# Three norms of a decoder trunk: the last tile's squares are added on VectorE and summed by one product, a step later

## The chip, the cores and the metric

The kernel runs on one core of one Trainium2 chip. The metric is the device time of one execution in microseconds (us), as the median of several runs. A profiled execution of the same kernel gives the trace: for every instruction its engine, its line in the kernel, its start and its length.

Engines are named as in the trace: PE is TensorE's matmuls and PEld its weight loads, DVE is VectorE, ACT is ScalarE, POOL is GpSimd, SP is SyncE.

## What is computed

A trunk of two decoder layers over 512 tokens of width 1024: a gated short convolution, a squared-ReLU MLP, then an attention layer that reads a shared key/value cache, and a second MLP. Each part starts with an RMS norm over the 1024 channels. Three of these norms matter here: the one before the first MLP (norm 1), the one before the shared keys and values (norm 2) and the one before the second MLP (norm 3).

```python
def rms_norm(x, g):
    xf = x.astype(jnp.float32)
    y = xf * lax.rsqrt(jnp.mean(xf * xf, axis=-1, keepdims=True) + EPS)
    return y.astype(x.dtype) * g
...
        x = x + g_m[:, None, :] * y
        h = modulate(rms_norm(x, norm_mlp_g[l]), sh_f, sc_f)
        x = x + g_f[:, None, :] * squared_relu_mlp(h, mlp_w1[l], mlp_w2[l])
        if l == N_A - 1:
            k, v, F = shared_kv(x, kv_norm_g, w_kv, k_norm_g, w_f, b_f)
```

## The kernel before

**Layout.** Channels lie on the 128 partitions, so `x` is eight tiles of 128 channels by 512 tokens, and a sum over channels is a sum over the eight tiles and over the partitions. Every dense product is made in three matmuls of rounded parts (`products`, lines 734 to 736): high weights by high activations, high by low, low by high. Each weight block therefore needs a high part (ScalarE, line 1299) and a low part (VectorE, line 1828), and so does each tile of `h` (`h_hi` from ScalarE, `h_lo` from VectorE).

**A norm in two token halves.** To keep TensorE at work across a norm, the last three blocks (`SPLIT = 3`) of the dense stage ahead of it are computed for tokens 0 to 255 first, then for tokens 256 to 511, and so is the norm. For each half ScalarE squares a tile into `tb` and VectorE adds it to `ssum` (`half_add`, line 1921). The last tile's squares are not added: `norm_sum` multiplies `ssum` by a matrix of ones (line 773) and then `tb`, which holds the last squares, by the same ones (line 775), both unrounded float32 into one bank. This gives every partition the sum over all channels. ScalarE then makes the root by a logarithm and an exponential (`norm_root`, line 1331 and the two after it), VectorE refines it (`norm_end`, lines 1857, 1860 and 1861), scales the tiles (line 1873, in norm 2 line 1886), ScalarE writes the high part and VectorE the low part (line 1882, in norm 2 line 1891).

**The order on TensorE.** `first_blocks` takes the stage behind the norm. For the first half it runs k from 0 to 10: at k it gives block 0 its tile k (`step(0, half, k)`, three matmuls of 128x256) and block 1 its tile k-3. Each step waits until that tile's low part is there (`h_ok`). At k = 5, ahead of the step, stands `norm_sum(n, 1)`, the sum of the second half. Then comes a third block over the first half (24 matmuls), and only then the steps of the second half, which need the second root. In norm 2 block 0 is the forget gate's (`wf_hi`, `wf_lo`).

**The order on VectorE.** `norm_in_halves` runs, for each half, low part m, then the scaling of tile m+2. In the first half it puts in the updates of `x` for the second half (line 1912, after m = 0, 2, 4) and the additions of squares (line 1921, after m = 2 and 4). After m = 7 it waits for the second root. In norm 1 and 2 the low part of the third or the next weight block (line 1828) stands behind the first two scalings of the second half; norm 2 has another one ahead of `norm_end`.

**The order on ScalarE.** `norm_in_halves` there runs the high parts of the 16 half tiles, with the squares of the second half ahead of m = 2, 4 and 6, and the second root ahead of m = 8.

All queues run in program order; semaphores join them.

Of the kernel before, what the change touches and what calls it, by code (L numbers as in the profile page):

```python
# [23 lines left out]
ALU = mybir.AluOpType  # L24
# [6 lines left out]
KT = D // P  # L31
# [77 lines left out]
def yoco_trunk(nc, x_in, c_in, ada_w, ada_b, norm_mix_g, norm_mlp_g, sc_w_in, sc_conv, sc_w_out,  # L109
# [13 lines left out]
    def new(name, shape, dt):  # L123
        offset = top[0]
        top[0] += size(shape, dt)
        return at(name, shape, dt, offset)
# [6 lines left out]
    def stacked(offset, specs):  # L133
        made = []
        for name, shape, dt in specs:
            made.append(at(name, shape, dt, offset))
            offset += size(shape, dt)
        return made
# [46 lines left out]
    ssum = new("ssum", [P, T], F32)  # L185
# [4 lines left out]
    tb, = stacked(region_tb, [("tb", [P, 2, T], F32)])  # L190
# [15 lines left out]
    ones = new("ones", [P, P], F32)  # L206
# [9 lines left out]
    cols = new("cols", [P, ROWS], F32)  # L216
# [58 lines left out]
    with ExitStack() as ctx:  # L275
# [3 lines left out]
        def sem(name):  # L279
            return ctx.enter_context(nc.semaphore(name))  # L280
# [39 lines left out]
        half_done = sem("half_done")  # L320
        half_ok = sem("half_ok")
        sq_half = sem("sq_half")
        ss_ok = sem("ss_ok")
        norm_pe = sem("norm_pe")
        norm_y = sem("norm_y")
# [75 lines left out]
        HALF = [slice(0, T // 2), slice(T // 2, T)]  # L401
        HALF_OUT = [slice(0, T), slice(T, 2 * T)]
        ALL = slice(0, T)
        SPLIT = 3
        SQ = [None] + [n * (KT - 1 + SPLIT - 1) for n in range(3)]

        def norm_no(n, half):

            return 2 * n - 1 + half if n else 0
# [320 lines left out]
        def _(pe):  # L730
            mm, turn = nc.tensor.matmul, nc.tensor.transpose

            def products(out, weights_hi, weights_lo, hi, lo, k, cols=ALL):
                mm(out[:, cols], weights_hi, hi[:, k, cols], start=(k == 0), stop=False)  # L734
                mm(out[:, cols], weights_hi, lo[:, k, cols], start=False, stop=False)  # L735
                return mm(out[:, cols], weights_lo, hi[:, k, cols], start=False, stop=(k == KT - 1))  # L736

            def part_of(b, s, out, hi, lo, tiles, ready=None, cols=ALL, weights=(w_hi, w_lo)):

                pe.wait_ge(lo_ok, b + 1)  # L740
                for k in tiles:
                    if ready:
                        ready(k)
                    last = products(out, weights[0][:, s, k, :], weights[1][:, s, k, :], hi, lo, k, cols)
                return last
# [21 lines left out]
            def norm_sum(n, half):  # L767

                out, cols = bank[4][:, 0:T // 2], HALF[half]
                pe.wait_ge(ss_ok, SQ[n] + KT - 1 + half * (SPLIT - 1))  # L770
                if half:
                    pe.wait_ge(norm_v, norm_no(n, 0) + 1)
                mm(out, ones[:], ssum[:, cols], start=True, stop=False)
                pe.wait_ge(sq_half, norm_no(n, half))
                mm(out, ones[:], tb[:, 1 - half, cols], start=False, stop=True).then_inc(norm_pe, 1)
# [22 lines left out]
            def first_blocks(base, targets, n, third):  # L798


                def step(which, half, k):
                    out, weights_hi, weights_lo, done, split_at = targets[which]
                    pe.wait_ge(h_ok, base + half * KT + k + 1)
                    if k == 0 and half == 0:
                        pe.wait_ge(*split_at)
                        if which:
                            pe.wait_ge(half_ok, SPLIT * (n - 1) + 1)
                    last = products(out, weights_hi(k), weights_lo(k), h_hi, h_lo, k, HALF[half])
                    if half and k == KT - 1:
                        last.then_inc(done, 1)  # L810

                for half, lag in ((0, 3), (1, 3)):
                    for k in range(KT + lag):
                        if half == 0 and k == 5:
                            norm_sum(n, 1)
                        if k < KT:
                            step(0, half, k)
                        if k >= lag:
                            step(1, half, k - lag)
                    if half == 0:  # L820
                        b, out = third
                        pe.wait_ge(half_ok, SPLIT * (n - 1) + 2)
                        part_of(b, b % GROUP, out, h_hi, h_lo, range(KT), cols=HALF[0])
# [991 lines left out]
        def _(dve):  # L1815
            steps = [0]
            tt, stt, ts = nc.vector.tensor_tensor, nc.vector.scalar_tensor_tensor, nc.vector.tensor_scalar
# [97 lines left out]
            def half_add(n, half, i):  # L1915

                m = SQ[n] + KT - SPLIT + i + half * (SPLIT - 1)
                dve.wait_ge(sq_ok, m + 1)
                dve.wait_ge(ss_ok, m)
                cols = HALF[half]  # L1920
                tt(ssum[:, cols], ssum[:, cols], tb[:, (i + 1 + half) % 2, cols], ALU.add).then_inc(ss_ok, 1)

            def norm_in_halves(n, b, layer, part, scale, low):

                half_tile(n, 0, SPLIT - 1, b, layer, part)
                half_add(n, 0, SPLIT - 2)
                if n == 1:
                    ada_step(b // GROUP, b % GROUP, KT - 1, 5)
                    split((b + 2) // GROUP, (b + 2) % GROUP)
                if n == 3:  # L1930
                    split((b + 3) // GROUP, (b + 3) % GROUP)
                norm_end(n, 0, HALF[0])
                for half in range(2):
                    first = half * KT
                    for m in range(first, first + 2):
                        scale(m, m % KT, HALF[half])
                    if half and n != 3:
                        split((b + 3) // GROUP, (b + 3) % GROUP)
                    for m in range(first, first + KT):
                        low(m, m % KT, HALF[half])  # L1940
                        if m in (0, 2, 4):
                            half_tile(n, 1, m // 2, b, layer, part)
                        if m in (2, 4):
                            half_add(n, 1, m // 2 - 1)
                        if m + 2 < first + KT:
                            scale(m + 2, (m + 2) % KT, HALF[half])
                    if half == 0:
                        if n == 2:
                            split((b + 2) // GROUP, (b + 2) % GROUP)
                        norm_end(n, 1, HALF[1])  # L1950
# [257 lines left out]
            def mlp(layer, first, g_base):  # L2208
# [39 lines left out]
                with dve.Fori(1, CH - 1) as c:  # L2248
# [9 lines left out]

            mlp(0, MLP0, G_MLP0)
            norm_in_halves(2, KVQ - 1, 0, 5, lambda m, j, part: times_rms(H_KV + m, j, part),  # L2260
                           lambda m, j, part: kv_low(H_KV + m, j, part))

# [306 lines left out]
            for c in range(LAST):  # L2569
                n, nxt, last = GROUP * (c + 1), c + 1, c == LAST - 1  # L2570
# [80 lines left out]
```

## Time and profile before

| | us |
|---|---|
| median of 3 runs | 1168.93 |
| lowest and highest | 1168.38, 1169.27 |
| profiled execution, device time | 1169.95 |
| its span in the trace | 1168.2 |
| PE busy | 1150.4 |
| DVE busy | 872.1 |
| ACT busy | 547.1 |

The profiled execution took 1.02 us more than the median, and 1.75 us of it lie outside the span. A row of the trace below has the start in us from the start of the span, the length, the engine, the line, the operation and its output and inputs. Matmuls overlap: the length of one includes filling and emptying the array, so the pace is read from one start to the next. The same holds on VectorE and ScalarE, where the next operation often starts a little before the end of the one ahead.

### The profile page before, as it was taken

Reading aid. Unit: us, or ns where it says so; the run is one execution under the profiler, and the core shown is the slowest. Engines: PE = TensorE matmul, PEld = TensorE weight load, DVE = VectorE, ACT = ScalarE, POOL = GpSimd, SP = SyncE. Lnnn points to the kernel's source line nnn. Section 1 sums busy time; section 2 is a strip of 40 time slices with the busy share of each in tenths; the row PEclk is TensorE's granted clock in tenths of the full one; section 3 lists DMA queues with packets and bytes.
Section 4 is the critical chain, followed back from the end, with each engine's and each line's share of the span. In section 5 each row is a group of like instructions: output and inputs, shape, how many; then the busy total and the mean of one; then the engine's idle time right before and its main releaser. Section 6 shows DMA issues by size and latency. Waiting matters only on the chain.

```text
span 1168.2 us, 16194 instructions
## 1 busy us (share of the span) xinstructions
PE 1150.4 (98%) x5751; PEld 965.3 (83%) x5751; DVE 872.1 (75%) x1188; ACT 547.1 (47%) x874; POOL 25.2 (2%) x37
## 2 busy tenths in 40 slices
PE   6999999999999999999999999999999999999998
PEld 4788888988888888888978888888988888888887
DVE  5656888886675675545889888897887777769694
ACT  5422333642232241233678778774675344545521
POOL 2000000000000000200020000000000000000000
PEclk9999999999999999999999999999999999999999
DMA  9767566376666656333255455464033323332311
GB/s 327 249 184 251 172 206 199 109 216 197 189 189 197 198 179 198 109 91 90 64 136 132 123 131 139 111 163 142 24 106 124 95 88 109 108 113 86 109 55 72
DMA packets 200987, 168.87 MB, mean 145 GB/s; under 512 B 5620, under 2 KB 173724, under 8 KB 200924
## 3 DMA queue, kind: packets, MB, share of 16 engines
q1 hardware_dynamic: 200732, 167.92, 48.1%
q8 instruction: 38, 0.62, 0.2%
q14 instruction: 25, 0.20, 0.1%
q10 hardware_dynamic: 160, 0.06, 0.0%
q0 software_dynamic: 32, 0.07, 0.0%
HBM read 153.24 MB, written 2.10 MB: 133 GB/s over the span
## 4 chain that ended last, share of the span: by engine, by line
PE 91%; DVE 5%; ACT 2%; issue 1%; DMA 1%; SPq 0%; DVEq 0%; ACTq 0%
PE bank L734 23%; PE bank L736 23%; PE bank L735 23%; PE bank L991 4%; PE bank L989 4%; PE bank L990 4%; PE bank L1141 1%; PE bank L1159 1%; PE bank L1131 1%; PE bank L1132 1%; DMA x_rows<-in_x 1%; PE bank L866 1%; DVE w_lo L1828 0%; PE bank L856 0%; DVE neg_max L2316 0%
## 5 line engine op out<-in xcount | busy, mean ns | idle before, releaser
L734 PE MATMUL bank<-h_hi,w_hi 128*128 128x512 f32 (+1 forms) x864 | 325.1, 376 | 2.1 <-DVE w_lo L1828 2.1
L736 PE MATMUL bank<-h_hi,w_lo 128*128 128x512 f32 (+1 forms) x864 | 322.7, 374 | 0.0
L735 PE MATMUL bank<-h_lo,w_hi 128*128 128x512 f32 (+1 forms) x864 | 322.7, 373 | 0.0
L1299 ACT ACTIVATE w_hi<-raw 128x1024 fp32r<-128x1024 f32 x151 | 158.5, 1054 | 151.7 <-DMA raw<-in_mlp_w 114.7
L1828 DVE TENSOR_TENSOR w_lo<-raw,w_hi 128x1024 fp32r<-128x1024 f32 x151 | 183.6, 1220 | 38.7 <-ACT w_hi L1299 37.9
L734 PEld LDWEIGHTS bank<-h_hi,w_hi 128*128 128x128 f32 x864 | 162.7, 188 | 30.7 <-issue 2.9
L736 PEld LDWEIGHTS bank<-h_hi,w_lo 128*128 128x128 f32 x864 | 162.7, 188 | 28.9
L735 PEld LDWEIGHTS bank<-h_lo,w_hi 128*128 128x128 f32 x864 | 162.8, 188 | 28.5 <-issue 0.2
L734 PE MATMUL bank<-g_hi,w_hi 128*128 128x512 f32 (+1 forms) x416 | 154.9, 372 | 0.0
L736 PE MATMUL bank<-g_hi,w_lo 128*128 128x512 f32 (+1 forms) x416 | 153.5, 369 | 0.0
L735 PE MATMUL bank<-g_lo,w_hi 128*128 128x512 f32 (+1 forms) x416 | 153.4, 369 | 0.0
L2107 DVE SCALAR_TENSOR_TENSOR ada_acc<-ada_raw,c_act,ada_acc 128x1024 f32<-128x1024 f32 (+1 forms) x80 | 102.2, 1277 | 0.4
L735 PEld LDWEIGHTS bank<-g_lo,w_hi 128*128 128x128 f32 x416 | 78.5, 189 | 13.3 <-issue 0.2
L736 PEld LDWEIGHTS bank<-g_hi,w_lo 128*128 128x128 f32 x416 | 78.4, 188 | 13.3
L734 PEld LDWEIGHTS bank<-g_hi,w_hi 128*128 128x128 f32 x416 | 78.4, 188 | 12.9 <-issue 0.2
L1583 ACT ACTIVATE w_hi<-w_raw 128x1024 fp32r<-128x1024 f32 x53 | 55.7, 1054 | 43.2 <-DVE w_raw L2539 17.3
L2155 DVE SCALAR_TENSOR_TENSOR x<-bank,mod,x 128x512 f32 (+1 forms) x39 | 29.1, 747 | 58.6 <-PE bank L736 57.7
L2530 DVE TENSOR_TENSOR y_acc<-bank,y_acc 128x1024 f32<-128x1024 f32 x38 | 46.3, 1217 | 29.6 <-PE bank L991 29.6
L1515 ACT ACTIVATE ta<-bank 128x512 f32<-128x512 f32 x32 | 19.1, 596 | 98.4 <-PE bank L736 98.4
L2516 DVE TENSOR_TENSOR w_lo<-w_raw,w_hi 128x1024 fp32r<-128x1024 f32 x53 | 64.5, 1217 | 0.0
L2213 DVE TENSOR_TENSOR tb<-ta 128x512 f32<-128x512 f32 x32 | 22.1, 692 | 48.0 <-ACT ta L1515 48.0
L989 PE MATMUL bank<-w_hi,ga_hi 128*128 128x512 f32 x144 | 56.8, 394 | 0.0
(271 smaller groups left out, 1690.3 us busy)
## 6 DMA issues: line engine op xcount, KB each, us to landing
raw<-in_mlp_w SPq DMA_DIRECT2D x96, 512.0 KB, 3.9
ada_raw<-in_ada_w SPq DMA_DIRECT2D x40, 1024.0 KB, 5.3
w_raw<-in_mlp_w SPq DMA_DIRECT2D x32, 512.0 KB, 3.2
raw<-in_sc_w_in SPq DMA_DIRECT2D x20, 512.0 KB, 4.1
ada_first<-in_ada_w SPq DMA_DIRECT2D x32, 256.0 KB, 7.9
raw<-in_w_kv SPq DMA_DIRECT2D x16, 512.0 KB, 3.8
raw<-in_q_w SPq DMA_DIRECT2D x8, 512.0 KB, 4.6
keys<-qk SPq DMA_DIRECT2D x16, 256.0 KB, 3.1
```

The source lines that it names most:

```text
L734: mm(out[:, cols], weights_hi, hi[:, k, cols], start=(k == 0), stop=False)
L735: mm(out[:, cols], weights_hi, lo[:, k, cols], start=False, stop=False)
L736: return mm(out[:, cols], weights_lo, hi[:, k, cols], start=False, stop=(k == KT - 1))
L989: mm(out, g_high, w_high, start=start, stop=False, skip_group_check=True)
L990: mm(out, g_high, w_low, start=False, stop=False, skip_group_check=True)
L991: return mm(out, g_low, w_high, start=False, stop=True, skip_group_check=True)
L1299: go(w_hi[:, jj, :, :], raw[:, jj, :, :], ACT.Copy).then_inc(hi_ok, 1)
L1583: go(w2_hi[:, s, :, :], w2_raw[:, s, :, :], ACT.Copy).then_inc(pair_hi_ok[PAIR_OF[name]], 1)
L1828: tt(w_lo[:, jj, :, :], raw[:, jj, :, :], w_hi[:, jj, :, :], ALU.subtract).then_inc(lo_ok, 1)
L2107: stt(out=acc, in0=ada_raw[:, s, half * D:(half + 1) * D], scalar=col(c_act, k), in1=acc, op0=ALU.mult, op1=ALU.add).then_inc(ada_used, 1)
L2516: tt(w2_lo[:, s, :, :], w2_raw[:, s, :, :], w2_hi[:, s, :, :], ALU.subtract).then_inc(pair_ok[PAIR_OF[name]], 1)
L2530: one = tt(to, of, to, ALU.add)
```

## The change

In the second half of each of the three norms, VectorE adds the last tile's squares to `ssum` as well (`last_add`), behind low part m = 6 and ahead of low part m = 7. It waits for the square (`sq_half`) and for the addition before it (`ss_ok`), and raises a new semaphore, `last_added`. TensorE's `norm_sum(n, 1)` is now one product, `ssum` by ones; it waits for `last_added` and is issued at k = 6 in place of k = 5. The first half is as before.

```diff
             def norm_sum(n, half):
 
                 out, cols = bank[4][:, 0:T // 2], HALF[half]
-                pe.wait_ge(ss_ok, SQ[n] + KT - 1 + half * (SPLIT - 1))
                 if half:
+                    pe.wait_ge(last_added, n)
                     pe.wait_ge(norm_v, norm_no(n, 0) + 1)
+                    mm(out, ones[:], ssum[:, cols], start=True, stop=True).then_inc(norm_pe, 1)
+                    return
+                pe.wait_ge(ss_ok, SQ[n] + KT - 1)
                 mm(out, ones[:], ssum[:, cols], start=True, stop=False)
                 pe.wait_ge(sq_half, norm_no(n, half))
                 mm(out, ones[:], tb[:, 1 - half, cols], start=False, stop=True).then_inc(norm_pe, 1)
...
-                        if half == 0 and k == 5:
+                        if half == 0 and k == 6:
                             norm_sum(n, 1)
...
+            def last_add(n):
+
+                cols = HALF[1]
+                dve.wait_ge(sq_half, norm_no(n, 1))
+                dve.wait_ge(ss_ok, SQ[n] + KT - 1 + SPLIT - 1)
+                tt(ssum[:, cols], ssum[:, cols], tb[:, 0, cols], ALU.add).then_inc(last_added, 1)
+
...
                         if m in (2, 4):
                             half_add(n, 1, m // 2 - 1)
+                        if m == 6:
+                            last_add(n)
                         if m + 2 < first + KT:
                             scale(m + 2, (m + 2) % KT, HALF[half])
```

TensorE in norm 2, before: the two products of the sum (L773, L775) stand ahead of step k = 5, whose first row is the one on `wf_hi` behind them.

```order
L736 MATMUL bank<-h_hi,w_lo 128x256
L773 MATMUL bank<-ssum,ones 128x256 [waits norm_v,ss_ok]
L775 MATMUL bank<-tb,ones 128x256 [waits sq_half]
L734 MATMUL bank<-h_hi,wf_hi 128x256 [waits h_ok]
L735 MATMUL bank<-h_lo,wf_hi 128x256
L736 MATMUL bank<-h_hi,wf_lo 128x256
L734 MATMUL bank<-h_hi,w_hi 128x256 [waits h_ok]
L735 MATMUL bank<-h_lo,w_hi 128x256
L736 MATMUL bank<-h_hi,w_lo 128x256
```

The same place now (its lines stand one or more further down in the file):

```order
L735 MATMUL bank<-h_hi,wf_hi 128x256 [waits h_ok]
L736 MATMUL bank<-h_lo,wf_hi 128x256
L737 MATMUL bank<-h_hi,wf_lo 128x256
L735 MATMUL bank<-h_hi,w_hi 128x256 [waits h_ok]
L736 MATMUL bank<-h_lo,w_hi 128x256
L737 MATMUL bank<-h_hi,w_lo 128x256
L774 MATMUL bank<-ssum,ones 128x256 [waits norm_v,last_added]
L735 MATMUL bank<-h_hi,wf_hi 128x256 [waits h_ok]
```

Step k = 5 has moved ahead of the sum, the second product is gone, and the sum waits for `last_added`. The last row is step k = 6.

VectorE in norm 3, before: from the second addition of squares (L1921) to the scaling of the second half. The two low parts in one row are m = 6 and m = 7.

```order
L1921 TENSOR_TENSOR ssum<-ssum,tb 128x256 [waits ss_ok,sq_ok]
L1873 SCALAR_TENSOR_TENSOR ta<-x,gains,rms 128x256 [waits h_ok]
L1882 SCALAR_TENSOR_TENSOR h_lo<-tc,mod,h_hi 128x256 [waits hh_ok]
L1873 SCALAR_TENSOR_TENSOR ta<-x,gains,rms 128x256 [waits h_ok]
L1882 SCALAR_TENSOR_TENSOR h_lo<-ta,mod,h_hi 128x256 [waits hh_ok] x2
L1857 SCALAR_TENSOR_TENSOR rms<-ty 128x256 [waits norm_y]
L1860 TENSOR_TENSOR rms<-rms,tc 128x256 [waits norm_v,vec_step]
```

And now:

```order
L1886 SCALAR_TENSOR_TENSOR h_lo<-ta,mod,h_hi 128x256 [waits hh_ok]
L1932 TENSOR_TENSOR ssum<-ssum,tb 128x256 [waits ss_ok,sq_half]
L1886 SCALAR_TENSOR_TENSOR h_lo<-ta,mod,h_hi 128x256 [waits hh_ok]
L1861 SCALAR_TENSOR_TENSOR rms<-ty 128x256 [waits norm_y]
L1864 TENSOR_TENSOR rms<-rms,tc 128x256 [waits norm_v,vec_step]
```

One addition (L1932) has come between low part 6 and low part 7; nothing else on VectorE has moved. ScalarE's order is unchanged.

## Rows read from the trace of the kernel before

**Rows 1.** The page: busy time by engine, and the chain that ended last.

```profile
PE 1150.4 (98%) x5751; PEld 965.3 (83%) x5751; DVE 872.1 (75%) x1188; ACT 547.1 (47%) x874; POOL 25.2 (2%) x37
...
PE 91%; DVE 5%; ACT 2%; issue 1%; DMA 1%; SPq 0%; DVEq 0%; ACTq 0%
```

**Rows 2.** Timeline of PE, norm 1: start, us, line, operation [idle before <- releaser].

```profile
213.81 0.60 PE L773 MATMUL bank<-ssum,ones 128*128 128x256 f32 x2
214.25 0.59 PE L775 MATMUL bank<-tb,ones 128*128 128x256 f32 x2
...
215.40 0.28 PE L734 MATMUL bank<-h_hi,w_hi 128*128 128x256 f32 x1
...
219.70 0.35 PE L734 MATMUL bank<-h_hi,w_hi 128*128 128x256 f32 x1 [1.63 <-DVE w_lo L1828]
```

**Rows 3.** Timeline of DVE, norm 1.

```profile
213.90 0.47 DVE L1882 SCALAR_TENSOR_TENSOR h_lo<-tc,mod,h_hi 128x256 fp32r<-128x256 f32 x1
214.30 0.47 DVE L1873 SCALAR_TENSOR_TENSOR ta<-x,gains,rms 128x256 f32<-128x256 f32 x1
214.70 0.47 DVE L1882 SCALAR_TENSOR_TENSOR h_lo<-ta,mod,h_hi 128x256 fp32r<-128x256 f32 x1
...
216.16 0.43 DVE L1857 SCALAR_TENSOR_TENSOR rms<-ty 128x256 f32<-128x256 f32 x1 [0.32 <-ACT ty L1332]
...
218.34 1.22 DVE L1828 TENSOR_TENSOR w_lo<-raw,w_hi 128x1024 fp32r<-128x1024 f32 x1
```

**Rows 4.** Line 1921, all of the program: count, ns least/median/most.

```profile
L1921 DVE TENSOR_TENSOR ssum<-ssum,tb x12: 408/414/418, 199.6 to 831.0; 128x256 f32<-128x256 f32 x12
```

**Rows 5.** Timeline of ACT, norm 1: the root of the second half.

```profile
215.22 0.45 ACT L1331 ACTIVATE ty<-bank,eps_col 128x256 f32<-128x256 f32 x1
```

**Rows 6.** Timeline of PE, norm 2: step 6, then steps 2 and 3 of half two.

```profile
569.96 0.28 PE L734 MATMUL bank<-h_hi,wf_hi 128*128 128x256 f32 x1
...
576.19 0.39 PE L734 MATMUL bank<-h_hi,wf_hi 128*128 128x256 f32 x1
576.41 0.28 PE L735 MATMUL bank<-h_lo,wf_hi 128*128 128x256 f32 x1
576.53 0.28 PE L736 MATMUL bank<-h_hi,wf_lo 128*128 128x256 f32 x1
576.92 0.39 PE L734 MATMUL bank<-h_hi,wf_hi 128*128 128x256 f32 x1
```

**Rows 7.** Timeline of DVE, norm 2.

```profile
568.81 0.47 DVE L1891 SCALAR_TENSOR_TENSOR h_lo<-x_rms,cols,h_hi 128x256 fp32r<-128x256 f32 x1
...
571.00 0.42 DVE L1857 SCALAR_TENSOR_TENSOR rms<-ty 128x256 f32<-128x256 f32 x1
...
576.38 0.48 DVE L1891 SCALAR_TENSOR_TENSOR h_lo<-x_rms,cols,h_hi 128x256 fp32r<-128x256 f32 x1
```

**Rows 8.** Timeline of ACT, norm 2: the root of the second half.

```profile
569.45 0.48 ACT L1331 ACTIVATE ty<-bank,eps_col 128x256 f32<-128x256 f32 x1
```

**Rows 9.** Timeline of PE, norm 3: step 6 of either half.

```profile
833.24 0.28 PE L734 MATMUL bank<-h_hi,w_hi 128*128 128x256 f32 x1
...
841.88 0.28 PE L734 MATMUL bank<-h_hi,w_hi 128*128 128x256 f32 x1
```

**Rows 10.** Timeline of DVE, norm 3: low part 6 of either half.

```profile
832.51 0.48 DVE L1882 SCALAR_TENSOR_TENSOR h_lo<-ta,mod,h_hi 128x256 fp32r<-128x256 f32 x1
...
841.19 0.48 DVE L1882 SCALAR_TENSOR_TENSOR h_lo<-ta,mod,h_hi 128x256 fp32r<-128x256 f32 x1
```

**Rows 11.** Timeline of ACT, norm 3: the root of the second half.

```profile
833.04 0.46 ACT L1331 ACTIVATE ty<-bank,eps_col 128x256 f32<-128x256 f32 x1
```

**Rows 12.** Windows (us): length, busy us (count) of PE, PEld, DVE, ACT, POOL; PEclk, DMA share, GB/s.

```profile
20.00:30.00 10.00, 8.70 (x41) 5.63 (x42) 7.80 (x15) 5.31 (x8) 0.00 (x0) 0.83 1.09 356
210.00:222.00 12.00, 10.37 (x84) 10.09 (x83) 11.39 (x28) 7.44 (x16) 0.00 (x0) 1.00 0.58 173
```

More of the change, by code:

```diff
@@ L322, in yoco_trunk @@
         sq_half = sem("sq_half")
+        last_added = sem("last_added")
         ss_ok = sem("ss_ok")
```

## The prediction, made before the run

> **What bounds the kernel now.** I read the page first. PE is busy 98% of the span, and 91% of the chain that ended last is PE's [rows 1]. So whatever makes TensorE wait is paid in full, and matmul work taken off a stretch where TensorE never waits is gained in full. The edits lie in three short stretches, one for each norm, where TensorE's work on the first token half has to last until the second half is ready. For each I read the timelines of PE, VectorE and ScalarE side by side. In norm 1 the cover already fails: behind the first half TensorE stands idle 1.63 us until VectorE has the low part L1828 of the third block, whose matmul starts at 219.70 [rows 2]. That low part starts at 218.34, behind the refinement that starts at 216.16 [rows 3], which goes back to ScalarE's logarithm at 215.22 [rows 5] and so to the sum. In norm 2 TensorE waits for single low parts of the second half: a step starts at 576.92 [rows 6], 0.06 us after the low part that ends at 576.38 + 0.48 = 576.86 [rows 7]. In norm 3 TensorE doesn't wait: step 6 of the second half starts at 841.88 [rows 9], and its low part has ended at 841.19 + 0.48 = 841.67 [rows 10]. With 0.06 us for the signal that leaves 0.15 us of slack.
>
> **What is removed.** The second product of the second half's sum, in three places. Its price is the distance from L773 to L775, 214.25 - 213.81 = 0.44 us [rows 2], so 3 x 0.44 = 1.32 us of TensorE. That is the whole gain there is; it counts only where TensorE doesn't wait afterwards.
>
> **What is added.** Three additions of 128x256, each like L1921 with 0.41 us [rows 4], on VectorE. Low part 7 behind each starts at most 0.1 us later, since it had waited for ScalarE; VectorE's own time isn't the cost. The cost is the moment at which the sum can start. Before, both inputs of the sum were there when TensorE came to it, and TensorE reached it without a pause. Now it needs an addition that stands behind low part 6.
>
> **Norm 1, step by step.** TensorE is free for step 5 at 213.81, where the sum stood [rows 2]. Low part 5 ends at 213.90 + 0.47 = 214.37 [rows 3], so step 5 starts at 214.37 + 0.06 = 214.43. The first matmul after such a wait takes 0.22 us to the next one (576.19 to 576.41) where the pace is 0.12 (576.41 to 576.53) [rows 6]: 0.10 us more. Six matmuls at 0.12 are behind: TensorE stands at the sum at 214.43 + 0.10 + 0.72 = 215.25. VectorE starts low part 6 at 214.70 [rows 3] and the operation behind such a one 0.40 later (213.90 to 214.30) [rows 3], so the addition runs from 215.10 to 215.51. The square that it reads is no bound: ScalarE makes it ahead of high part 6, for which low part 6 has waited. The sum is let go at 215.51 + 0.06 = 215.57, and **TensorE waits 0.3 us with all its queue behind it**. The product takes 0.60 us from start to end [rows 2], and 0.10 more as the first after a wait: it ends at 216.27, and with another 0.06 the logarithm starts at 216.33 where it started at 215.22 [rows 5]: **1.11 us later**. Nothing between it and TensorE's restart has slack: refinement, scalings and L1828 follow one upon the other up to 219.70. TensorE's own path is late by less: step 6 starts at 215.57 + 0.10 + 0.44 = 216.11 where it started at 215.40 [rows 2], 0.71 us, and the idle stretch covers that. So norm 1 costs 1.11 us, and the 0.44 us of the removed product are lost in a longer wait: 1.63 + 1.11 - 0.71 = 2.0 us.
>
> **Norm 2.** Low part 6 starts at 568.81 [rows 7]; the addition ends at 568.81 + 0.40 + 0.41 = 569.62, the sum starts at 569.68, ends at 570.38, and the logarithm starts at 570.44 where it started at 569.45 [rows 8]. From the logarithm to the refinement it is 216.16 - 215.22 = 0.94 us [rows 3, 5], so VectorE could start at 571.38. It started at 571.00 [rows 7], since it had a weight's low part to finish first: here most of the delay is covered, and **0.38 us** are left. They go on to every low part of the second half, for which TensorE waits already. TensorE's own path (step 6 at 569.68 + 0.10 + 0.44 = 570.22 for 569.96 [rows 6]) is late by 0.26 and doesn't decide.
>
> **Norm 3.** Low part 6 starts at 832.51 [rows 10]: addition until 833.32, sum from 833.38 to 834.08, logarithm at 834.14 for 833.04 [rows 11], 1.10 us later. TensorE's own path: step 6 at 833.38 + 0.10 + 0.44 = 833.92 for 833.24 [rows 9], 0.68 us late. The second half's low part 6 ends at 841.67 + 1.10 = 842.77 and lets its step go at 842.83, where TensorE started it at 841.88: 0.95 us, and 0.10 for the first matmul after a wait. **1.05 us.**
>
> **The sum.** 1.11 + 0.38 + 1.05 = 2.54 us. What follows each norm is TensorE's chain again, so I let the shifts add. On the profiled execution that is a span of 1168.2 + 2.5 = 1170.7 us and 1169.95 + 2.5 = 1172.5 us in all; this execution lay 1.02 above the median, and on the median it is 1168.93 + 2.5 = 1171.4 us. The term that no row shows is an unrounded product directly behind a wait. Below, it costs no more than in a stream: without the 0.10 in the three releases and in norm 3's step the terms are 1.01, 0.28 and 0.85, together 2.1 us. Above, two passes (the x2 of L773) could each be 0.10 late: 1.21, 0.48 and 1.15, together 2.8 us. I take the middle, since the late first matmul is what the two waits nearest in kind show.
>
> The rows show that extra 0.10 us because weights and matmul both start only after the wait. The Trainium skill ("TensorE: Matmul & The Clock Gate", Part 2, what happens when a matmul is issued) says that TensorE pulls weight loads ahead of matmuls in flight. By that rule alone the ones would lie in the array before the wait ends, and the sum would be the lower one, 2.1 us; the rows speak against it where the wait stands ahead of the load.
>
> **Rivals.** *Cover.* The change could be not slower but faster: if the addition lands before TensorE comes to the sum, there is no wait, and the logarithm, which ScalarE couldn't start before its high part 7 anyway, is hardly later. The place is the release at 215.57 against TensorE's arrival at 215.25. It decides at 0.3 us: were VectorE that much earlier or TensorE that much later, TensorE would lose nothing of its own, and with a covered root it gains up to 1.32 us: 1168.9 - 1.3 = 1167.6. Against it: moving the sum behind step 5 alone makes it late, because step 5 waits for its own low part until 214.43, and in norm 1 no part of the root's delay has cover. *Slack.* In norm 3 the second half hides more than I read, TensorE pays only its own 0.68 or less, and the lateness in norm 1 is nearer to its own path too: 0.71 + 0.28 + 0.5 = 1.5, so 1170.4. For it speaks that the slack in norm 3 is read from one step. *Clock.* The idle stretch in norm 1 grows from 1.63 to 2.0 us. Between 20 and 30 us, where TensorE was busy 8.70 of 10 us, the granted clock was 0.83, between 210 and 222 us, with the idle stretch in it, 1.00 [rows 12]. A mean of 0.83 over 10 us is 3.4 us at the lower of the two levels (1.2 in place of 2.4 GHz), which loses half of them, 1.7 us: 2.5 + 1.7 gives 1173.1. Against it: nearly the same stretch did nothing to the clock before. The Trainium skill (the same page, Part 1, the clock gate) says that an idle TensorE falls to half its clock; the early window agrees with it, the norm before doesn't show it. That the change doesn't do what it says is out: the order of instructions shows the product gone and the addition there.
>
> **How the numbers follow.** The forecast's mechanism has 0.76. What a measurement of this kernel can tell from no change is about 0.2%, 2.34 us, so the threshold lies at 1171.27, just below my 1171.4 and inside the bounds 1171.0 to 1171.7: of the 0.76 I give 0.45 to slower by over 0.2% and 0.31 to within. Slack has 0.12 and Cover 0.05, both within 0.2%; Clock has 0.05, slower. The last 0.02 are for a gain of over 2.34 us, for which I see no source. Faster 0.02, same 0.48, slower 0.50. The range goes from just under Slack to just under Clock, 1170.2 to 1172.8. It holds the forecast's bounds with room for the measurement (the runs before are 0.9 us apart) and leaves Cover and Clock out.
>
> **What would show it.** Right: a wait of TensorE of about 0.3 us ahead of L774 in the norms, with the addition L1932 as its releaser; the logarithm 1.1 us later behind low part 6 in norms 1 and 3 and 1.0 in norm 2; norm 1's idle stretch at 2.0 us; new waits of TensorE for low parts in norm 3's second half. Wrong: no wait ahead of L774, or a span under 1169.5, which would say that the root isn't what TensorE waits for; a granted clock below 1.00 behind norm 1; or a different end of the addition than 0.8 us behind the start of low part 6.

## The result and the profile after

| | before | changed |
|---|---|---|
| median, us (8 runs each) | 1168.96 | 1172.15 |
| lowest and highest | 1168.38, 1169.37 | 1171.15, 1173.84 |
| profiled execution | 1169.95 | 1171.40 |
| its span | 1168.2 | 1169.6 |

The change makes the kernel slower: the ratio is 1.003 with a 95% interval of 1.0021 to 1.0038, 3.2 us by the medians (2.5 to 4.4 us by the interval). The forecast was 1171.4 and the range 1170.2 to 1172.8. The two profiled spans differ by only 1.4 us, because the start of the program differs from one execution to the next: TensorE begins norm 1's first half at 211.29 in the trace before and at 209.87 in this one. So the norms are compared by stages, not by the span.

The page of the changed kernel, the rows that answer to [rows 1]:

```profile
PE 1149.4 (98%) x5745; PEld 964.3 (82%) x5745; DVE 873.1 (75%) x1191; ACT 547.6 (47%) x874; POOL 25.3 (2%) x37
...
PE 87%; DVE 8%; ACT 2%; issue 1%; DMA 1%; SPq 1%; DVEq 0%; ACTq 0%
```

TensorE has six matmul records less (two for each product) and VectorE three instructions more. PE is busy 1.0 us less, and yet its share of the chain that ended last has gone from 91 to 87%; VectorE's has gone from 5 to 8%. The end of the program now hangs on VectorE for longer.

Norm 1 of the changed kernel, timelines of PE, DVE and ACT in turn (start, us, engine, line). They answer to [rows 2, 3, 5]:

```profile
213.00 0.38 PE L735 MATMUL bank<-h_hi,w_hi 128*128 128x256 f32 x1 [0.45 <-DVE h_lo L1886]
...
214.13 0.70 PE L774 MATMUL bank<-ssum,ones 128*128 128x256 f32 x2 [0.16 <-DVE ssum L1932]
...
219.71 0.36 PE L735 MATMUL bank<-h_hi,w_hi 128*128 128x256 f32 x1 [2.38 <-DVE w_lo L1832]
```

```profile
213.26 0.47 DVE L1886 SCALAR_TENSOR_TENSOR h_lo<-ta,mod,h_hi 128x256 fp32r<-128x256 f32 x1
213.66 0.42 DVE L1932 TENSOR_TENSOR ssum<-ssum,tb 128x256 f32<-128x256 f32 x1
...
215.82 0.42 DVE L1861 SCALAR_TENSOR_TENSOR rms<-ty 128x256 f32<-128x256 f32 x1 [1.35 <-ACT ty L1336]
216.63 0.42 DVE L1864 TENSOR_TENSOR rms<-rms,tc 128x256 f32<-128x256 f32 x1 [0.38 <-DVE rms L1861]
```

```profile
214.86 0.48 ACT L1335 ACTIVATE ty<-bank,eps_col 128x256 f32<-128x256 f32 x1 [0.98 <-PE bank L774]
```

Step 5 now waits for its low part (0.45 us), the sum waits for the addition L1932, and ScalarE waits 0.98 us for the sum. The addition ends at 213.66 + 0.42 = 214.08, 0.82 us behind the start of low part 6 (0.8 was forecast). From low part 6 to the logarithm it is 214.86 - 213.26 = 1.60 us, where it was 215.22 - 214.70 = 0.52: 1.08 us later. The last two VectorE rows show something that the trace before doesn't have: L1864 starts 0.81 us behind L1861, where the same pair stood 0.46 apart in norms 2 and 3 and in the kernel before. VectorE stands idle 0.38 us ahead of it with its inputs there: L1861 ended at 216.24, and ScalarE had written `tc` by 216.16. This is called the stall below.

Norms 2 and 3, PE then DVE then ACT, for [rows 6, 7, 8, 9, 10, 11]:

```profile
569.68 0.70 PE L774 MATMUL bank<-ssum,ones 128*128 128x256 f32 x2
```

```profile
571.37 0.43 DVE L1861 SCALAR_TENSOR_TENSOR rms<-ty 128x256 f32<-128x256 f32 x1 [0.22 <-ACT ty L1336]
```

```profile
570.42 0.47 ACT L1335 ACTIVATE ty<-bank,eps_col 128x256 f32<-128x256 f32 x1 [0.98 <-PE bank L774]
```

```profile
832.68 0.39 PE L735 MATMUL bank<-h_hi,w_hi 128*128 128x256 f32 x1 [0.43 <-DVE h_lo L1886]
...
833.81 0.70 PE L774 MATMUL bank<-ssum,ones 128*128 128x256 f32 x2
...
843.26 0.37 PE L735 MATMUL bank<-h_hi,w_hi 128*128 128x256 f32 x1
```

```profile
842.70 0.48 DVE L1886 SCALAR_TENSOR_TENSOR h_lo<-ta,mod,h_hi 128x256 fp32r<-128x256 f32 x1
```

In norm 3 step 6 of the second half starts at 843.26, 0.08 us behind the end of its low part (842.70 + 0.48 = 843.18): TensorE, which didn't wait there before, now goes at VectorE's pace. Counted from the first step of norm 3, that step 6 starts 0.95 us later than before (13.69 us for 12.74).

In this trace the granted clock was 1.00 from 219.70 to 225.00 us, behind norm 1's idle stretch of 2.38 us.

**The stages of all kernels.** From the start of the first step of a norm's first half to a fixed matmul behind the norm, in one profiled execution each: norm 1 to the restart behind the idle stretch, norm 2 to the first sum of the key heads, norm 3 to the first matmul of 128x512. Such a difference doesn't depend on how the program started. "Norm 1 to 2" and "norm 2 to 3" are the stretches between. In us:

| kernel | norm 1 | its idle stretch | norm 1 to 2 | norm 2 | norm 2 to 3 | norm 3 |
|---|---|---|---|---|---|---|
| before | 8.41 | 1.63 | 346.16 | 18.75 | 244.53 | 18.14 |
| changed | 9.84 | 2.38 | 346.15 | 19.13 | 244.58 | 19.17 |
| changed, again | 9.84 | 2.38 | 346.15 | 19.14 | 244.63 | 19.17 |
| change in norm 1 only | 9.83 | 2.37 | 346.15 | 18.75 | 244.51 | 18.14 |
| change in norms 2 and 3 only | 8.41 | 1.63 | 346.15 | 19.13 | 244.57 | 19.16 |
| only the move | 9.51 | 2.04 | 346.17 | 19.20 | 244.59 | 19.18 |
| addition earlier | 9.45 | 2.38 | 346.16 | 18.81 | 244.56 | 18.77 |
| product at k = 5 | 9.83 | 1.65 | 346.17 | 19.11 | 244.58 | 19.53 |
| idle stretch filled | 9.83 | 0.93 | 346.17 | 19.12 | 244.56 | 19.16 |
| root late, no change | 9.36 | 2.58 | 347.66 | 18.73 | 244.52 | 18.14 |
| addition beside | 8.41 | 1.62 | 346.16 | 18.81 | 244.50 | 18.14 |
| changed, padded | 9.49 | 2.04 | 346.16 | 19.12 | 244.54 | 19.15 |
| low part first in norm 1 | 7.62 | 0.83 | 346.18 | 18.74 | 244.51 | 18.14 |
| and last in norm 2 | 7.62 | 0.84 | 346.18 | 18.15 | 245.18 | 18.14 |

The change costs 1.43 + 0.38 + 1.03 = 2.84 us in the three norms, and nothing between them. Behind norm 3 the spans go on for 320.86 to 320.94 us in all of these executions, so what is left to differ lies ahead of norm 1: its first step starts between 209.62 and 211.29 us.

### The profile page after: what moved, and what is told of

Read it like the earlier page. It is cut to its first block, busy times and chain, and to the rows that moved or that the text cites. A ratio compares the mean times of both kernels' runs of the same rounds, so it can differ in the third digit from the quotient of the medians.

```text
span 1169.6 us, 16188 instructions
## 1 busy us (share of the span) xinstructions
PE 1149.4 (98%) x5745; PEld 964.3 (82%) x5745; DVE 873.1 (75%) x1191; ACT 547.6 (47%) x874; POOL 25.3 (2%) x37
## 4 chain that ended last, share of the span: by engine, by line
PE 87%; DVE 8%; ACT 2%; issue 1%; DMA 1%; SPq 1%; DVEq 0%; ACTq 0%
PE bank L735 23%; PE bank L737 22%; PE bank L736 22%; PE bank L995 4%; PE bank L994 4%; PE bank L993 4%; PE bank L1145 1%; PE bank L1163 1%; PE bank L1135 1%; DVE w_lo L1832 1%; DMA first_raw<-in_sc_w_in 1%; PE bank L1136 1%; DVE neg_max L2329 1%; SPq L449 0%; DVE h_lo L1886 0%
```

## The experiments

Medians are of 7 to 11 runs each; the kernel before ran beside them, with a median of 1168.85 us (28 runs) for the first four, 1169.33 (29 runs) for the next four and 1168.67 (32 runs) for the last four. Each 95% interval is about 2 us wide, so differences between two changed kernels are read from the stages.

### The changed kernel again

No edit.

> The changed kernel once more, for another profile and more times. Theory (the root of the second half is late, and in some executions the granted clock falls behind the longer idle stretch of norm 1): times in two groups, near 1171.4 us with a granted clock of 0.999 and 1.0 to 1.7 us above with 0.997 or less; median 1171.4 to 1172.5. Rival (the extra time is scatter of the start or of DMA): times spread evenly and the granted clock at 0.999 in all of them.

Measured: 1171.92 us, 3.1 over before, ratio 1.0025 (1.0015 to 1.0035), from 1171.21 to 1172.44. The stages repeat within 0.05 us, the stall between L1861 and L1864 included. Two of nine executions had a granted clock of 0.997, seven 0.999, but the times of the two, 1172.19 and 1172.44, lie only just above the others. No second group is to be seen here. In the eight executions of the result it looked otherwise: four at 0.999 took 1171.15 to 1171.82 us and four at 0.997 or less 1172.49 to 1173.84. But the kernel before has executions at 0.997 too (23 of 89), and in the set of 29 they lie 1.0 us above those at 0.999 (medians 1169.55 and 1168.55), so a clock of 0.997 doesn't belong to the change.

### In which norm

```diff
-                if half:
+                if half and n in (1,):
...
-                        if half == 0 and k == 6:
+                        if half == 0 and k == (6 if n in (1,) else 5):
...
-                        if m == 6:
+                        if m == 6 and n in (1,):
```

The other kernel has `(2, 3)` in place of `(1,)`.

> The change in norm 1 alone, norms 2 and 3 as before. Theory: 1.1 us for the late root, and the clock's share, if there is one, comes with it whole, since the longer idle stretch is here: 1170.1 at a clock of 0.999 and 1171.5 to 1171.8 at 0.997; in the trace the same idle stretch of 2.0 to 2.4 us. Rival (the scatter comes from all three places or from none): all executions at 1170.1.

> The change in norms 2 and 3 alone, norm 1 as before. Theory: 0.38 + 1.05 = 1.4 us, 1170.4 us, with no second group of times and a granted clock of 0.999, since norm 1's idle stretch stays at 1.63 us. Rival (scatter has nothing to do with norm 1): the same spread of 2 to 3 us as the changed kernel.

Measured: 1170.36 us (1.5 over before) and 1170.20 us (1.35 over). By stages 1.42 in norm 1 for the one, 0.38 and 1.02 for the other: the costs add up, and none touches another norm. Both kernels had a spread of 1.2 us, no wider than the 2.0 of the kernel before beside them. So norm 1 alone didn't bring a second group of times; and its 1.42 us are 0.3 more than the root's delay of 1.1, which left the stall to be explained.

### Only the move

```diff
-                        if half == 0 and k == 5:
+                        if half == 0 and k == 6:
```

> Only the move: the sum of the second half at k = 6 with its two products, no addition of the last squares. Theory: TensorE reaches the sum at 215.25 by norm 1's clock, both inputs are there, the two products take 0.44 + 0.59 us and end at 216.28, so the logarithm is as late as in the changed kernel (1.1 us) and the time the same within 0.4 us: 1171.5 to 1172.5. Rival (the addition on VectorE and the wait for it are what costs): with no addition the time is within 0.6 us of before.

Measured: 1171.49 us, 2.6 over before, ratio 1.0026 (1.0015 to 1.0036). By stages 1.10 + 0.45 + 1.04 = 2.59 us. With no addition and no wait for it, the move alone costs nearly as much as the whole change. The rival falls. The reason is the one of the expectation: once the sum stands behind step 5, TensorE gets there late, and the second product (0.43 us from start to start in this trace) takes as long as the wait for the addition (0.32) and the late first matmul (0.10) together. The stall between L1861 and L1864 is absent here (norm 1 has 9.51, idle stretch 2.04).

### The addition earlier

```diff
-                        if m == 6:
-                            last_add(n)
                         if m + 2 < first + KT:
                             scale(m + 2, (m + 2) % KT, HALF[half])
+                        if m == 5:
+                            last_add(n)
```

> The changed kernel with the addition of the last squares one place earlier on VectorE, behind the scaling of tile 7 and ahead of low part 6. Theory: the addition ends before TensorE comes to the sum, so the wait is gone and only the move is left: logarithm 0.7 us late in norms 1 and 3, norm 2 at 0.1, together 1.4 us or 1170.3, 1.0 us or more faster than the changed kernel. Rival (the wait for the addition costs nothing, since TensorE's idle stretch covers it): no gain over the changed kernel.

Measured: 1170.84 us, 1.5 over before. Each against its own runs of before, that is 1.6 to 1.7 less than the changed kernel; by stages it is 1.1 less. Norm 2 costs 0.06 and norm 3 0.63, near what was expected; norm 1 costs 1.04, of which the stall, still there, is 0.35. The wait for the addition therefore costs about 0.4 us in norm 1 (1.43 - 1.04), 0.3 in norm 2 and 0.4 in norm 3 on top of the move. With one product less and no wait for the addition the kernel is still slower than before: the move isn't earned back. Against only the move, where the sum also starts without a wait, the removed product does show: norm 1 without the stall is 0.41 us shorter (9.51 against 9.45 - 0.35), norm 2 0.39 and norm 3 0.41. That is its price of 0.44 us three times over, gained because the root comes earlier.

### The product at k = 5

```diff
-                        if half == 0 and k == 6:
+                        if half == 0 and k == 5:
```

> The changed kernel with its one product at k = 5, where the sum stood. TensorE waits for the addition with steps 5 and 6 behind it. Theory (the root's delay decides in norm 1, TensorE's own path in norm 2): the root is as late as in the changed kernel, norm 1 again 1.1, norm 2 0.9 to 1.0 because TensorE itself is 1.3 us late less 0.44, norm 3 1.1 to 1.4: 3.1 to 3.5 us, 1172.0 to 1172.4. Rival (the place of the product is what costs): near before, 1169.5.

Measured: 1172.23 us, 2.9 over before. By stages 1.42, 0.36 and 1.39. Norm 1 costs the same as with the product at k = 6 although its idle stretch is back at 1.65 us: there only the root's delay counts. Timeline of PE of this kernel, norm 1:

```profile
213.88 0.70 PE L774 MATMUL bank<-ssum,ones 128*128 128x256 f32 x2 [1.58 <-DVE ssum L1932]
```

The expectation for norm 2, 0.9 to 1.0, was wrong. TensorE itself decides there, as expected: it enters the second half 0.96 us late (10.46 us behind norm 2's first step, for 9.50). But before it had lost 0.6 us waiting for low parts at steps 2 and 3 of that half [rows 6], and now it is late enough to wait at neither, so 0.36 remains. That the root's delay is nearly the same, 0.38, is a coincidence. In norm 3, where there were no such waits, TensorE's own lateness comes through (1.39).

### The granted clock: the idle stretch filled, and the root late without the change

```diff
                         b, out = third
+                        if n == 1:
+                            pe.wait_ge(half_ok, SPLIT * n)
+                            for _ in range(12):
+                                mm(bank[3][:, HALF[0]], w_hi[:, 0, 0, :], h_hi[:, 0, HALF[0]], start=True, stop=True)
```

> The changed kernel with twelve more matmuls of 128x256 on TensorE in norm 1's idle stretch, between the steps of the first half and the third block, into a bank that is free then; their result is used by nothing. They take 1.44 us of a stretch of 2.0 to 2.4 us, so no time of their own. Theory (the granted clock falls in some executions behind the longer idle stretch): the executions 1 to 2 us above the lowest go away, 1171.4 with a spread of 1.5 us. Rival (scatter of another source): the spread stays at 2 to 3 us and the median within 0.3 us of the changed kernel's.

Measured: 1172.21 us, 2.9 over before, from 1171.09 to 1172.91. The idle stretch is down to 0.93 us, the stages are those of the changed kernel, and so, within the noise, is the median; the spread of 1.8 us lies between the 1.2 and the 2.7 of the changed kernel's two sets. The rival holds. So the clock behind norm 1 isn't what makes the typical execution of the changed kernel slower than the forecast.

The other kernel is the one before, with the root of norm 1 made late on VectorE:

```diff
                     if half == 0:
+                        if n == 1:
+                            for _ in range(3):
+                                link(tt(rms[:, HALF[1]], x[:, 0, HALF[1]], x[:, 1, HALF[1]], ALU.add))
```

> The kernel before with three more additions on VectorE in norm 1 ahead of the refinement of the second root, one waiting for the other; they write into a half tile that the refinement overwrites. They push the refinement from 216.2 to 217.2 by norm 1's clock. Theory: what counts is the root's delay and the idle stretch, not the change: 1.0 us or 1169.9, with an idle stretch of 2.6 us, and in some executions a lower granted clock behind it and 1.4 us more. Rival (the change's own instructions make the scatter): all executions at 1169.9 with the spread of before.

Measured: 1170.54 us, 1.2 over before, but in two groups: five executions from 1169.25 to 1169.70 with a granted clock of 0.998, and five from 1171.47 to 1172.68, four of them at 0.996 or less. One lies between. The groups lie 2.4 us apart by their medians, more than the fall of the clock described here costs. The profiled execution was one of the upper group, with a mean clock of 0.995. Its PE timeline, then its windows (us: length, busy us of PE, PEld, DVE, ACT, POOL, PEclk):

```profile
220.22 0.55 PE L734 MATMUL bank<-h_hi,w_hi 128*128 128x256 f32 x1 [2.58 <-DVE w_lo L1828]
220.57 0.41 PE L735 MATMUL bank<-h_lo,w_hi 128*128 128x256 f32 x1
220.78 0.41 PE L736 MATMUL bank<-h_hi,w_lo 128*128 128x256 f32 x1
...
223.56 0.32 PE L734 MATMUL bank<-h_hi,w_hi 128*128 128x256 f32 x1
223.71 0.28 PE L735 MATMUL bank<-h_lo,w_hi 128*128 128x256 f32 x1
223.83 0.28 PE L736 MATMUL bank<-h_hi,w_lo 128*128 128x256 f32 x1
```

```profile
210.00:220.00 10.00, 7.64 (x61) 7.33 (x59) 9.61 (x24) 6.12 (x13) 0.00 (x0) 1.00 0.61 203
220.00:225.00 5.00, 4.78 (x27) 4.81 (x28) 5.00 (x14) 2.69 (x6) 0.00 (x0) 0.66 0.00 0
```

Behind an idle stretch of 2.58 us TensorE ran 3.3 us (220.22 to 223.56) at the lower level, 1.2 GHz: 0.21 us from matmul to matmul in place of 0.12. From 225 to 240 us the granted clock was 1.00 again. The stretch from norm 1 to norm 2 was 347.66 us in place of 346.16, so this fall cost 1.50 us; the forecast's rival had put 1.7. The same execution also had a lower clock near its start (0.72 between 20 and 30 us, where the traces before and after the change have 0.83); so did the profiled execution of the next kernel, whose mean clock was 0.997 and whose stages are those of before. So in these two traces a mean of 0.997 came with the start alone, and 0.995 with the start and the fall behind norm 1. The Trainium skill ("TensorE: Matmul & The Clock Gate", Part 1, the clock gate) says that an idle TensorE drops to half its clock; this trace agrees.

### The addition beside

The kernel before with the third addition at the changed kernel's place, written where the refinement overwrites it; only the refinement waits for it. Sum and product stay as before.

```diff
+            def last_add(n):
+
+                cols = HALF[1]
+                dve.wait_ge(sq_half, norm_no(n, 1))
+                dve.wait_ge(ss_ok, SQ[n] + KT - 1 + SPLIT - 1)
+                tt(rms[:, cols], ssum[:, cols], tb[:, 0, cols], ALU.add).then_inc(last_added, 1)
...
+                        if m == 6:
+                            last_add(n)
...
+                if half:
+                    dve.wait_ge(last_added, n)
                 refine_start(rms[:, cols], ty[:, 0, cols])
```

> The kernel before with the third addition of the second half at the place where the changed kernel has it, in all three norms, but written into the half of rms that the refinement overwrites, so that the sum doesn't need it; the sum stays at k = 5 with two products. Theory: VectorE's own time for the addition is no cost (low part 7 up to 0.1 us later); if the stall of 0.35 us between L1861 and L1864 in norm 1, which every kernel with the addition there shows and no other, comes from the additional instructions on VectorE and not from the late root, it is here too and costs up to 0.35 us: 0.1 to 0.4 us over before. Rival (the stall comes with the late root): no stall, within 0.1 us of before. Rival (the addition itself is what costs): 1 us or more over before.

Measured: 1168.89 us, 0.2 over before, ratio 1.0001 (0.9992 to 1.001). The stages are those of before, but for 0.06 us in norm 2. The addition as such costs next to nothing. The stall isn't there. This kernel has one wait more ahead of the pair in norm 1 than the changed kernel, so the pair doesn't lie at the same place of VectorE's stream.

### The changed kernel, padded

```diff
             def norm_in_halves(n, b, layer, part, scale, low):
 
+                if n == 1:
+                    for _ in range(8):
+                        dve.wait_ge(consts, 1)
```

> The changed kernel with eight waits that are fulfilled long since on VectorE ahead of norm 1, so that its instructions there lie at other places in its stream. Theory (the stall of 0.35 us between L1861 and L1864 in norm 1 is a matter of where the instructions lie): the stall is gone or has moved to another instruction, norm 1's idle stretch 2.0 us in place of 2.4, and the time up to 0.35 us lower than the changed kernel. Rival (it belongs to the two instructions and their waits): the stall stays at 0.35 us between the same two.

Measured: 1171.48 us, 2.8 over before (ratio 1.0025, 1.0016 to 1.0035). Timeline of DVE of this kernel, the same two rows in norm 1:

```profile
216.09 0.43 DVE L1861 SCALAR_TENSOR_TENSOR rms<-ty 128x256 f32<-128x256 f32 x1 [1.35 <-ACT ty L1336]
216.56 0.42 DVE L1864 TENSOR_TENSOR rms<-rms,tc 128x256 f32<-128x256 f32 x1
```

They are 0.47 us apart again, norm 1 costs 1.08 in place of 1.43, and the idle stretch is 2.04 us. Instructions that do nothing, put in ahead, take the stall away, with the addition and the late root still there. So neither of these is enough for it, and where the two instructions lie in VectorE's stream decides; one padding was tried. The stall is read from profiled executions only: the medians, 2.8 us over before here and 3.1 in the repeat of the changed kernel, agree with it, but can't tell 0.3 us.

### The low parts of the weight blocks moved

The stages show what norm 1 waits for: the low part of the third block. It stands behind two scalings that it doesn't need.

```diff
+                    if half and n == 1:
+                        split((b + 3) // GROUP, (b + 3) % GROUP)
                     for m in range(first, first + 2):
                         scale(m, m % KT, HALF[half])
-                    if half and n != 3:
+                    if half and n == 2:
                         split((b + 3) // GROUP, (b + 3) % GROUP)
```

> The kernel before with one thing moved in norm 1: the low part of the third block (L1828) ahead of the two scalings of the second half, not behind them. Theory (norm 1's idle stretch ends by that low part): TensorE restarts two scalings or 0.8 us earlier, and the low parts of the second half, 0.3 us later, still come in time: 0.8 us faster than before, with an idle stretch of 0.8 to 0.9 us in place of 1.63. Rival (TensorE then waits for the low parts of the second half instead): within 0.2 us of before, with new waits of TensorE between 222 and 227 us.

Measured: 1168.00 us against 1168.67 for before, ratio 0.9996 (0.9987 to 1.0005). By stages norm 1 is 0.79 us shorter, the time of the two scalings, and nothing is given back. Timeline of PE:

```profile
217.75 0.36 PE L734 MATMUL bank<-h_hi,w_hi 128*128 128x256 f32 x1 [0.83 <-DVE w_lo L1828]
```

The medians differ by 0.67 us, which the interval can't tell from nothing; the stage can.

The second kernel also puts norm 2's weight block behind all low parts of the second half (its edit against the kernel just above):

```diff
-                    if half and n == 2:
-                        split((b + 3) // GROUP, (b + 3) % GROUP)
                     for m in range(first, first + KT):
...
                             scale(m + 2, (m + 2) % KT, HALF[half])
+                    if half and n == 2:
+                        split((b + 3) // GROUP, (b + 3) % GROUP)
```

> As split_first, and in norm 2 the low part of the weight block that stands ahead of the second half's low parts goes behind all of them; that block is used only 12 us later. Theory (in norm 2 TensorE waits for the second half's low parts): they come 1.15 us earlier, the waits at its steps 2 and 3 go, 0.4 to 0.6 us; together with norm 1's 0.8 us 1.2 to 1.4 us faster than before. Rival (the weight's low part, or what VectorE does behind it, becomes late): no gain over split_first.

Measured: 1167.91 us, ratio 0.9994 (0.9985 to 1.0003), the same as split_first. Norm 2 is 0.60 us shorter, as expected, but the stretch from norm 2 to norm 3 is 0.65 us longer. One row tells where it went. Timeline of PE of split_first and of this kernel, the sum of a later head:

```profile
595.71 1.13 PE L1100 MATMUL bank<-tb,ones_head 128*128 128x512 f32 x2 [0.34 <-ACT tb L1663]
```

```profile
596.23 1.13 PE L1100 MATMUL bank<-tb,ones_head 128*128 128x512 f32 x2 [0.92 <-ACT tb L1663]
```

Counted from the first step of norm 2, TensorE was 0.56 us earlier at the matmul ahead of that sum (30.49 us for 31.05), but the sum started at the same moment (31.80 for 31.78), because ScalarE's squares came no earlier: it waited 0.92 us in place of 0.34, and the gain became a wait 13 us later.

## Why the prediction was right, point by point

**The removed product.** PE's busy time fell by 1.0 us for 1.32 forecast by starts, and in the changed kernel none of it showed: the move alone cost 2.59 us by stages, the whole change 2.84, or 2.49 without the stall. The forecast had counted the 0.44 us only where TensorE doesn't wait afterwards. The addition moved earlier shows that this was too narrow: there the product's 0.4 us are gained in each norm, although TensorE waits afterwards, because the product stands in the chain to the root. In the changed kernel the wait for the addition takes its place.

**Norm 1.** The root's delay was forecast at 1.11 us; the trace has 1.08, and the padded kernel, without the stall, costs 1.08. The wait ahead of the sum was forecast at 0.3: from the last matmul's start at 213.69 the sum would have started at 213.81 and started at 214.13, 0.32 later. The idle stretch was forecast at 2.0; it is 2.04 in the padded kernel. What the forecast didn't have is the stall of 0.35 us between L1861 and L1864, which makes norm 1 cost 1.43 and the stretch 2.38.

**Norm 2.** Forecast 0.38, measured 0.38. Sum, logarithm and refinement were forecast at 569.68, 570.44 and 571.38; the trace, which happens to be at the same time there, has 569.68, 570.42 and 571.37.

**Norm 3.** Forecast 1.05, measured 1.03. The parts hold as well: step 6 of the second half came 0.95 us later, as forecast, by the root and not by TensorE's own path.

**The late first matmul.** This was the unmeasured term. A product directly behind a wait takes 0.70 us from start to end, where two records in a stream take 0.60 [rows 2]: the 0.10 us is there once, not for both records of the product. The trace of the changed kernel has the load of the ones at 214.13, with the product's own start and not ahead of it. Had they been loaded ahead, 0.60 would be expected.

**The sum.** 2.54 us forecast, 2.84 us by stages, and 2.49 without the stall. So the three norms came out as forecast, and the 0.3 us between 2.54 and 2.84 is the stall, a term that the forecast didn't have. The medians say 3.2 and 3.1 in two sets of runs, with intervals of 2.5 to 4.4 and 1.8 to 4.1 us, so they agree with 2.84 and with 2.54. The start of the program makes up part of their scatter: norm 1's first step starts anywhere from 209.62 to 211.29 us, and the granted clock between 20 and 30 us was 0.83 in some traces and 0.72 in others. In the result half of the changed kernel's executions were at 0.997 or less, in the repeat two of nine. The executions at 0.999 alone give 1171.88 - 1168.92 = 2.96 us in the repeat's set.

**The rivals.** *Cover* fell, and the addition moved earlier shows why: even with no wait ahead of the sum the kernel is 1.5 us over before. That comparison still has the stall in it, so 1.4 us by stages is what the move costs with one product. *Slack* fell: norm 3 paid what the one step had said. *Clock* exists as a mechanism: the kernel with a late root shows it at 2.58 us of idle time, at 1.50 us. For the changed kernel itself it is only made likely. An execution at a clock of 0.996 or less occurred in 6 of 57 executions of the kernels whose idle stretch is 2.0 to 2.4 us (one of them is the 1173.84 of the result), and in none of the 62 with a stretch of 0.8 to 1.65 us; none of the six was profiled. From the fall that was profiled, 3.3 us at half the clock in 1170 us, I estimate 0.0014 off the mean clock; in an execution at 0.999 that would hardly stand out from the 0.997 that other causes give, so six may be too few. It isn't what moves the median as far as the runs can tell, since filling the stretch did not. The forecast had given it 0.05.

**The chances.** 0.50 for slower by over 0.2% and 0.48 for within it, from a threshold 0.1 us below the forecast. Without the stall the stages give 2.49 us, 0.15 above the threshold of 2.34 and well inside the scatter of a median. The outcome was 0.3%, with an interval that begins at 0.21%, just above the threshold. That it came out on this side is in part luck: the stall, which the forecast didn't have, and the scatter of the starts pushed it there.

## What to carry to other kernels

When a reduction feeds a latency chain that a saturated engine later waits for, the moment at which its input is complete is worth more than the engine's work in it: here 0.44 us of TensorE work was removed three times, and the root came up to 1.1 us later. The product's 0.4 us was worth having only once its input was there in time (the addition earlier). Before moving a product behind the next step, read whether that step has its inputs at that time; the step whose wait the product had hidden now waited 0.45 us, and the move alone cost 2.6 us where the whole change cost 2.8. Read such a change stage by stage, from one fixed instruction to another, since a stage repeated to 0.05 us where single executions scattered by 1 to 2 us and the medians of the kernel before by 0.7.

## What the runs showed that I had not expected

- VectorE stalled for 0.35 us between two instructions, with its inputs there. It showed in six profiled executions of five kernels, all that had the addition feeding the sum in norm 1 without padding, always between the same two instructions and always with 0.80 to 0.81 us between their starts. It was gone with eight waits put in ahead, in the kernel with the addition beside and in those without an addition. The cause stays open. The loading of instructions is one candidate: in all six executions the trace has one DMA packet of the kind "instruction" (0.01 MB) on queue 14 between 217 and 218 us, 1.5 to 1.7 us behind the start of the first of the pair. But the kernel with only the move has one at 1.6 us too, without a stall, so the packets alone don't decide it.
- An idle stretch of 2.58 us can be enough for TensorE's granted clock to fall, but not in every execution: five of eleven were slower by about 2 us, four of them at a clock of 0.996 or less, and one of these was profiled. None of the 89 executions of the kernel before with a listed clock, whose stretch is 1.63 us, was at 0.996 or less.
- Work added into an idle stretch of TensorE (1.44 us of matmuls) changed no stage, and the median not beyond the noise.
- TensorE's lateness can vanish into waits that it would have had anyway: with the product at k = 5 it was 0.96 us late in norm 2 and paid 0.36.
